# A decoder trunk with a mixture of experts on one core: the last projection with tokens stationary, a router by K quarters, fp32r counts, and three moved steps

## The chip, the core and the metric
The kernel runs on one core of a Trainium2 chip and is written engine by engine: TensorE (PE, with PEld for its weight loads), VectorE (DVE), ScalarE (ACT), GpSimd (POOL) and SyncE (SP, which mostly issues DMAs). Engines meet through semaphores. The metric is the device time of one execution in microseconds (us). Before the change three runs gave 897.81 us in the median (897.41 to 899.27).

## The reference
One layer over 320 tokens (256 of a prompt, 64 of 8 samples), width 2048, all fp32:

```
h = x @ w_in;  b, c, hc, u, v, p = split(h)
y = concat(b * conv3(c * hc), u * chunk_mix(LN(v)), pool(p))
x = LN(ALPHA * x + y @ w_out)                      # LN1
g = top1(softmax(x @ rg_w + rg_b))                 # one of 4 groups
e = top2(softmax((x @ re_w + re_b)[g]))            # 2 of its 4 experts
x = LN(ALPHA * x + sum_e gate_e * (silu(x @ w_gate_e) * (x @ w_up_e)) @ w_down_e)   # LN2
```

The outputs are x for all tokens and a few rows of state (the last rows of the convolution's and the pooling's inputs, the normalised v of the samples).

## The kernel before
**Projections.** A product with `w_in` or `w_out` is made from two parts of each operand: hi is the fp32r rounding, lo the rest, and hi*hi + hi*lo + lo*hi are summed in PSUM. A chunk of weights is 1 MB. SP loads it to `raw` (a ring of three, each load waits until the chunk three before it is used, `w_used`), ACT makes `w_hi` (L648), DVE `w_lo` (L656). `group_products` (L454) takes two chunks (8 K tiles by 256 columns each) with the weights stationary: per K tile and 128 columns three matmuls (L475 to L477) that stream the 320 tokens. A group fills two PSUM banks (pair g % 3); the result has the output columns on the partitions. Banks 6 and 7 are used in turn for transposes and small products (`tb_full`, `tb_free`). Groups 0 to 16 are `w_in`, groups 17 to 24 (G_O on) are `w_out`.

**The last projection.** Its input y is built in `tmp` two K tiles at a time by DVE, copied to `yT_hi` by ACT (`y_hi`, L680) and subtracted to `yT_lo` by DVE (`y_lo`, L816). The second half of K (tiles 8 to 15) comes first (HALF_O), since tiles 0 to 5 are only finished at its start. In ACT's program (`act_mixer`, g == 17) the order is: hi parts of chunks 34 and 35, `y_hi(2, 2)`, `y_hi(4, 2)`, the copies of z0 and z1 from banks 6 and 7 (L671), six small DMAs. On PE the transposes into z0 and z1 (L609) come right ahead of the projection. Since tokens are needed on the partitions afterwards, ACT copies each group to `mixT` (L793), PE turns it back (`out_tokens`, L624 and L629) and DVE adds it to ALPHA * x in `tok` (`residual`, L982 and L987) and takes its statistics (L996). Five of the expert units are loaded during this stage.

**LN1 and router.** LN1 is folded into the router: PE turns the unnormalised rows (48 transposes, L1142), ACT copies them to `zT` (L1356) with the root of the variance between its third and fourth copy, then PE multiplies all of K by the router's weights in four column strips (L1156, 32 instructions). DVE makes the choices. Cumulative counts of tokens per group and expert are fp32 matmuls with `before` and `ones` (`places_of`, L1169 to L1171, and L1183), the token that sits in each place comes from `group_slot` (L1177). DVE then writes `row` (L1448); POOL gathers the rows of group 0 from the copy in DRAM, `z_rows` (L1103), which has been stored by ACT (6 of 8 column groups) and SP (the last two).

**Experts.** The weights of 16 experts are 96 units of 2 MB (four of gate/up, two of down for each), in the order ORDER, in 11 slots. SP (`sp_experts`) issues units 5, 6, 9, 7, 10, 8 once the last projection is done, the fifth of them when `raw_made` is there, then unit 11 and so on, each when PE has used enough units (`ring_used`, `units_used`). For each expert PE turns the chosen rows (fill, L1206, with `order` from DVE's `pick`), multiplies by gate and up (L1270), turns the activation, multiplies by down (L1304) and combines with the gates (L1247). DVE's `normalise` (L1573) applies LN1 to the gathered rows, `finish` does LN2; its root is taken on ACT (`root`, L1405). POOL scatters the finished rows and gathers those of the group after the next one.

Of the kernel before, what the change touches and what calls it, by code (L numbers as in the profile page):

```python
# [37 lines left out]
def hybrid_trunk_kernel(nc, x_prompt, x_sample, state_conv, state_pool, w_in, conv_w, sgu_ln_g,  # L38
# [53 lines left out]
    BIG = 4096.0  # L92
# [30 lines left out]
    yT_hi = at("yT_hi", YT_HI0, [P, KT, NTOK], F32R)  # L123
    yT_lo = at("yT_lo", YT_LO0, [P, KT, NTOK], F32R)
# [35 lines left out]
    mixT = [at(f"mixT{s}", LATE + s * 2 * ROW, [P, 2, NTOK]) for s in range(3)]  # L160
# [9 lines left out]
    before = at("before", CO + 512, [P, P])  # L170
    ones = at("ones", CO + 1024, [P, P])
# [23 lines left out]
    group_slot = at("group_slot", G0 + 12 * KB, [P, 3, P])  # L195
# [39 lines left out]
    member = little("member", [P, 3, NR])  # L235
# [47 lines left out]
    small_out = S("small_out")  # L283
    copy_out = S("copy_out")
# [58 lines left out]
    HALF_O = (1, 0)  # L343
# [56 lines left out]
    def sp_program(sp):  # L400
# [18 lines left out]
        for o in range(16):  # L419
            c = 2 * G_O + o  # L420
            sp.wait_ge(w_used, c - RING + 1)
            h, col = HALF_O[o % 2], GW * (o // 2)
            sp.dma_start(raw[c % 3][:, :].rearrange("p (t n) -> p t n", t=CK),
                         wout_v[:, CK * h:CK * h + CK, col:col + GW]).then_inc(raw_full[c % 3], 16)
            if 4 <= o < 10:
                if o == 4:
                    sp.wait_ge(w_used, 2 * G_O)
                if o == 6:
                    sp.wait_ge(ylo_ready, 7)
                    sp.wait_ge(small_out, 16 * (4 + NB))  # L430
                load_half(sp, 2 + (o - 4) // 2, o % 2)

    def pool_program(pool):
        pool.memset(ident[:, :], 0.0).then_inc(pool_const, 1)
        pool.memset(ones[:, :], 1.0).then_inc(pool_const, 1)
# [7 lines left out]
        pool.affine_select(out=before[:, :], in_=ones[:, :], compare_op=ALU.is_gt, fill=0.0,  # L443
# [12 lines left out]
    def group_products(pe, g, acts, halves, turn=0, turns_at=0, wait_half=None, between=None):  # L456
# [6 lines left out]
        for n in range(2):  # L463
            if n and wait_half:
                pe.wait_ge(*wait_half)
# [47 lines left out]
    def pe_mixer(pe):  # L513
# [17 lines left out]
        X, Y = (xT_hi, xT_lo), (yT_hi, yT_lo)  # L531
# [81 lines left out]
        def out_tokens(k, turn=0):  # L613


            wait = pair_free[(G_O + k) % 3], (G_O + k) // 3 + 1 + turn
            pe.wait_ge(*wait)
            buf = mixT[k % 3]
            n = USE_O + 2 * k
            b, bank = bank_of(n, 3 * turn)  # L620
            b2, bank2 = bank_of(n + 1, 3 * turn)
            for i in range(2):
                for f in range(2):
                    last = pe.transpose(bank[:, GW * i + P * f:GW * i + P * (f + 1)],  # L624
                                        buf[:, f, P * i:P * (i + 1)], ident[:, :])
            last.then_inc(tb_full[b], 1)
            b, bank = b2, bank2
            for f in range(2):
                last = pe.transpose(bank[0:64, P * f:P * (f + 1)], buf[:, f, SEQ:NTOK], ident[:, :])  # L629
            last.then_inc(tb_full[b], 1)  # L630
# [28 lines left out]
    def store_z(eng, k, cols):  # L659

        for n in (USE_O + 2 * (k - 1), USE_O + 2 * (k - 1) + 1):
            b, full = tb(n)
            eng.wait_ge(tb_free[b], full)
# [3 lines left out]
    def act_mixer(act):  # L667
# [11 lines left out]
        def y_hi(first, n):  # L679
            act.activation(yT_hi[:, first:first + n, :], tmp[:, 0:n, :], ACT.Copy).then_inc(yhi_ready, 1)  # L680
# [105 lines left out]
        def copy_out_group(k, turn=0):  # L786
            g = G_O + k
            pair = g % 3
            act.wait_ge(w_used, 2 * g + 2 + 6 * turn)
            if k >= 3 or not isinstance(turn, int):  # L790
                b, full = tb(USE_O + 2 * k + 1)
                act.wait_ge(tb_full[b], full - 3 + 3 * turn)
            act.activation(mixT[k % 3][:, :, :], ps[:, 2 * pair:2 * pair + 2, 0:NTOK], ACT.Copy)\  # L793
               .then_inc(pair_free[pair], 1)

        with act.Fori(0, 2) as s:
            for i in range(3):
                split_hi(act, 2 * (G_O + 1 + i), s, 6)
                split_hi(act, 2 * (G_O + 1 + i) + 1, s, 6)
                copy_out_group(i, s)  # L800
        split_hi(act, 2 * G_END - 2)
        split_hi(act, 2 * G_END - 1)
        copy_out_group(6)
        store_z(act, 6, slice(0, 6 * GW))
        copy_out_group(7)

    def dve_mixer(dve):
# [6 lines left out]
        def y_lo(first, n, count):  # L814
            dve.wait_ge(yhi_ready, count)
            dve.tensor_tensor(yT_lo[:, first:first + n, :], tmp[:, 0:n, :],  # L816
                              yT_hi[:, first:first + n, :].bitcast(FP32), ALU.subtract)\
               .then_inc(ylo_ready, 1)
# [156 lines left out]
        def residual(k, turn=0):  # L975

            n = USE_O + 2 * k
            col = slice(GW * k, GW * (k + 1)) if isinstance(turn, int) else \
# [877 lines left out]
```

## Time and profile before

| | |
|---|---|
| median of three runs | 897.81 us |
| the profiled execution | 895.74 us |
| its span, first to last instruction | 894.0 us |
| PE busy | 837.3 us (94%) |
| DVE, ACT busy | 282.2 and 263.3 us |
| DMA: moved, mean rate | 267.80 MB, 300 GB/s |
| first part (`w_in`) | to 273 us |
| last projection | 273.4 to 391.1 us |
| LN1, router, first gather | 391 to 423 us |
| experts | 423 to 880 us |

The page gives the busy time of each engine and cuts the span in 40 slices of 22.35 us. The rows further down come from its views: a timeline gives start and length of merged neighbours ("x16" are 16 instructions) with the idle time before them and its releaser in brackets; windows give, for a stretch, the busy time and count of each engine, then the granted clock of PE (1.00 is 2.4 GHz, 0.50 is 1.2 GHz), the share of the DMA engines and GB/s; the chain of waits leads back from the last instruction.

### The profile page before, as it was taken

The numbers are of one execution on the slowest core, as the hardware profiler recorded it, in microseconds if no ns is written. First come the engines' busy times: TensorE is split into PE (matmuls) and PEld (weight loads), VectorE is DVE, ScalarE is ACT, GpSimd is POOL, SyncE is SP. The second block draws the span as 40 slices with busy tenths as digits, with TensorE's granted clock in tenths as the row PEclk, the third lists the DMA queues.
The fourth block names the chain that finished last, engine by engine and source line by source line (L and its number), as shares of the span: only waits on it lengthen the run. The fifth ranks groups of instructions, "written<-read, shape, count | busy, mean of one in ns | idle before, by whom it ended". The sixth has DMA issues, their size and how long they took to land.

```text
span 894.0 us, 11220 instructions
## 1 busy us (share of the span) xinstructions
PE 837.3 (94%) x4741; PEld 557.4 (62%) x4741; DVE 282.2 (32%) x388; ACT 263.3 (29%) x462; POOL 24.9 (3%) x41
## 2 busy tenths in 40 slices
PE   6999999999999999994999999998999989997993
PEld 6989999999999999984433333432333333333331
DVE  5383375335664444445000102043000330022203
ACT  5243332323223232321522332432223232222101
POOL 0000000000001000001000000000000000000000
PEclk9999999999999999995999999999999999999997
DMA  9644653654444884379898999999999999999980
GB/s 293 192 141 124 204 177 118 210 190 141 141 149 150 290 292 139 121 261 406 334 426 320 424 421 426 426 419 422 424 424 422 423 425 423 420 424 425 422 358 36
DMA packets 81148, 267.80 MB, mean 300 GB/s; under 512 B 5625, under 2 KB 58319, under 8 KB 59656
## 3 DMA queue, kind: packets, MB, share of 16 engines
q1 hardware_dynamic: 78042, 258.92, 74.7%
q0 software_dynamic: 1984, 5.31, 1.5%
q10 hardware_dynamic: 1078, 2.94, 1.0%
q8 instruction: 33, 0.54, 0.2%
q14 instruction: 11, 0.09, 0.0%
HBM read 263.07 MB, written 11.54 MB: 307 GB/s over the span
## 4 chain that ended last, share of the span: by engine, by line
PE 72%; DMA 15%; DVE 4%; ACT 4%; issue 2%; SPq 2%; POOL 0%; POOLq 0%; ACTq 0%; DVEq 0%
PE ps L1270 17%; PE ps L475 12%; PE ps L476 12%; PE ps L477 12%; PE ps L1304 9%; DMA down_w<-in_expert_w_down 4%; DMA gu_w<-in_expert_w_up 4%; DMA xg<-z_rows,row 4%; PE ps L1206 3%; DMA out<-xg,sample_row 3%; SPq L397 1%; ACT xT L1376 1%; DMA raw<-in_w_in 1%; DVE xg L1623 1%; PE ps L1247 1%
## 5 line engine op out<-in xcount | busy, mean ns | idle before, releaser
L1270 PE MATMUL ps<-gu_w,xT 128*64 128x512 f32 x1024 | 234.8, 600 | 7.7 <-DMA gu_w<-in_expert_w_up 6.7
L656 DVE TENSOR_TENSOR w_lo<-raw,w_hi 128x2048 fp32r<-128x2048 f32 x50 | 114.6, 2291 | 170.6 <-ACT w_hi L648 169.1
L475 PE MATMUL ps<-xT_hi,w_hi 128*128 128x320 f32 x512 | 159.2, 311 | 0.0
L477 PE MATMUL ps<-xT_hi,w_lo 128*128 128x320 f32 x512 | 158.2, 309 | 0.0
L476 PE MATMUL ps<-xT_lo,w_hi 128*128 128x320 f32 x512 | 158.2, 309 | 0.0
L1270 PEld LDWEIGHTS ps<-gu_w,xT 128*64 128x64 f32 x1024 | 71.5, 138 | 135.6 <-issue 131.2
L648 ACT ACTIVATE w_hi<-raw 128x2048 fp32r<-128x2048 f32 x49 | 93.8, 1915 | 207.9 <-DMA raw<-in_w_in 136.1
L1376 ACT ACTIVATE xT<-ps,gbT 128x64 f32<-128x64 f32 x256 | 82.4, 407 | 156.8 <-PE ps L1206 156.8
L1304 PE MATMUL ps<-down_w,aT 128*64 128x512 f32 x480 | 107.7, 601 | 4.5 <-ACT aT L1384 4.0
L475 PEld LDWEIGHTS ps<-xT_hi,w_hi 128*128 128x128 f32 x512 | 96.1, 188 | 0.5
L476 PEld LDWEIGHTS ps<-xT_lo,w_hi 128*128 128x128 f32 x512 | 96.1, 188 | 0.0
L477 PEld LDWEIGHTS ps<-xT_hi,w_lo 128*128 128x128 f32 x512 | 96.1, 188 | 0.0
L1645 DVE TENSOR_TENSOR a_sb<-ps,a_sb 128x256 f32<-128x256 f32 x16 | 6.8, 425 | 281.3 <-ACT a_sb L1428 281.3
L475 PE MATMUL ps<-yT_hi,w_hi 128*128 128x320 f32 x256 | 79.8, 312 | 0.7 <-DVE yT_lo L816 0.7
L1304 PEld LDWEIGHTS ps<-down_w,aT 128*64 128x64 f32 x480 | 33.3, 138 | 74.8 <-issue 61.9
L477 PE MATMUL ps<-yT_hi,w_lo 128*128 128x320 f32 x256 | 79.1, 309 | 0.0
L476 PE MATMUL ps<-yT_lo,w_hi 128*128 128x320 f32 x256 | 79.1, 309 | 0.0
L1206 PEld LDWEIGHTS ps<-order,xg 128*128 128x128 f32 x256 | 34.0, 196 | 57.5 <-issue 47.1
L1206 PE MATMUL ps<-order,xg 128*128 128x128 f32 x256 | 45.9, 305 | 8.6 <-DVE xg L1573 8.6
L475 PEld LDWEIGHTS ps<-yT_hi,w_hi 128*128 128x128 f32 x256 | 48.1, 188 | 0.9 <-DVE yT_lo L816 0.9
L476 PEld LDWEIGHTS ps<-yT_lo,w_hi 128*128 128x128 f32 x256 | 48.1, 188 | 0.0
L477 PEld LDWEIGHTS ps<-yT_hi,w_lo 128*128 128x128 f32 x256 | 48.0, 188 | 0.0
(257 smaller groups left out, 517.6 us busy)
## 6 DMA issues: line engine op xcount, KB each, us to landing
gu_w<-in_expert_w_gate SPq DMA_DIRECT2D x64, 1024.0 KB, 12.8
gu_w<-in_expert_w_up SPq DMA_DIRECT2D x64, 1024.0 KB, 15.0
down_w<-in_expert_w_down SPq DMA_DIRECT2D x32, 2048.0 KB, 19.6
raw<-in_w_in SPq DMA_DIRECT2D x34, 1024.0 KB, 5.3
raw<-in_w_out SPq DMA_DIRECT2D x16, 1024.0 KB, 5.3
tok<-in_x_prompt SPq DMA_DIRECT2D x2, 1024.0 KB, 6.4
z_rows<-tok ACTq DMA_DIRECT2D x2, 768.0 KB, 4.1
tok<-in_x_sample SPq DMA_DIRECT2D x1, 512.0 KB, 9.6
```

Source lines behind the costliest of these rows:

```text
L397: sp.dma_start(gu_w[s][:, n, :].rearrange("p (c f) -> p c f", c=4), src[:, e, h, c:c + 4, :])\
L475: pe.matmul(out, wh[:, t, col], hi[:, kt, :], start=(n == 0 and t == 0), stop=False)
L476: pe.matmul(out, wh[:, t, col], lo[:, kt, :], start=False, stop=False)
L477: last = pe.matmul(out, wl[:, t, col], hi[:, kt, :], start=False, stop=(n == 1 and t == CK - 1))
L648: act.activation(w_hi[k][:, :], raw[k][:, :], ACT.Copy).then_inc(hi_ready, 1)
L656: dve.tensor_tensor(w_lo[k][:, :], raw[k][:, :], w_hi[k][:, :].bitcast(FP32), ALU.subtract)\
L1206: last = pe.transpose(ps[:, fill_bank(e, j), P * c:P * (c + 1)], xg[g % 2][:, col:HD * (j // 2 + 1):HK], order[:, k, :])
L1247: last = pe.matmul(ps[:, ACC + 2 * h + q, :], gatedT[half, k, :], y[half, 512 * q:512 * (q + 1)], start=(k == 0), stop=(k == EG - 1))
L1270: last = pe.matmul(ps[C * side:C * (side + 1), GU, :], x, w[:, :, c, FH * side:FH * (side + 1)], start=(j == 0 and c == 0), stop=(j == PAI ...
L1304: last = pe.matmul(ps[C * side:C * (side + 1), out + q, :], turned[:, f % 2, f // 2, :], down_w[slot(i)][:, n, col:col + 512], start=(f == ...
L1376: last = act.activation(xT[e % 2][:, j, c, :], ps[:, fill_bank(e, j), P * c:P * c + C], ACT.Identity, bias=gbT[:, 1, j // 2, hc:hc + 1], s ...
L1623: dve.scalar_tensor_tensor(out=x[:, :], in0=x[:, :], scalar=zrstd[:, 0:1], in1=lnb[:, :], op0=ALU.mult, op1=ALU.add).then_inc(z_normed, 1)
```

## The change
- The last projection has the tokens stationary: `out_rows` goes over four quarters of 512 output columns; for each, four chunks of 4 K tiles by 512 columns. Tiles of 128 tokens: two of the prompt take three matmuls per K tile (hi with w_hi, lo with w_hi, hi with w_lo). The 64 sample tokens have their hi and lo parts side by side in `yT`, so that one stationary tile holds both, with two matmuls; DVE adds the two halves afterwards. The sums have the tokens on the partitions: no mixT copies, no `out_tokens`. `yT_hi` and `yT_lo` become one tensor with its K tiles placed by PLACE; `y_hi` and `y_lo` write it in pairs, `y_lo` in two pieces each.
- Residual and statistics go by quarters. PE waits for z0 and z1 to be read ahead of the first quarter, and for y's first six tiles ahead of the third chunk.
- Router: transposes go K quarter by K quarter, and the router's product of a quarter follows as soon as it is turned.
- `before`, `ones`, `member` and `group_slot` are fp32r, and the counts are fp32r matmuls; BIG is 512; the token numbers have a tensor of their own, `number`.
- SP waits for `xg_zero` 2 (POOL's clearing of the second xg, behind the first gather) ahead of unit 10.
- LN2's root is taken in `results`, ahead of the copies of gatedT and y, and the Silu table is called for once behind them; `pick` stands ahead of `normalise`.

```diff
+    yT = at("yT", YT_HI0, [P, KT, 2 * NTOK], F32R)
+    PLACE = (0, 1, 2, 8, 9, 10, 3, 4, 5, 11, 12, 13, 6, 7, 14, 15)
+    LO_S, LO_P = NTOK, 2 * NTOK - SEQ
-    HALF_O = (1, 0)
+    QUARTERS = (2, 3, 0, 1)
+    TO = 4
+    CO_W = CH // TO
+    QO = D // CO_W
+    ROW_BANKS = ((4, 5, 6), (0, 1, 7), (2, 3, 6), (4, 5, 7))
...
-        pe.wait_ge(ylo_ready, 4)
-        group_products(pe, G_O, Y, HALF_O, wait_half=(ylo_ready, 7))
-        with pe.Fori(0, 2) as s:
-            for i in range(3):
-                group_products(pe, G_O + 1 + i, Y, HALF_O, s, 3)
-                out_tokens(i, s)
-        group_products(pe, G_END - 1, Y, HALF_O)
-        out_tokens(6)
-        out_tokens(7)
+        wait_read(pe, "z0", "z1")
+        for q in range(QO):
+            out_rows(pe, q)
+
+    def out_rows(pe, q):
...
+        if q >= 2:
+            pe.wait_ge(rows_summed, 3 * (q - 1))
+        for n, kq in enumerate(QUARTERS):
+            c = 2 * G_O + 4 * q + n
+            if q == 0:
+                pe.wait_ge(ylo_ready, 4 if n < 2 else 7)
+            pe.wait_ge(lo_ready, c + 1)
...
+            for i in range(2):
+                out, rows = ps[:, ROW_BANKS[q][i], :], slice(P * i, P * (i + 1))
+                for t in range(TO):
+                    y = yT[:, PLACE[TO * kq + t], :]
+                    lo = slice(LO_P + P * i, LO_P + P * (i + 1))
+                    pe.matmul(out, y[:, rows], wh[:, t, :], start=(n == 0 and t == 0), stop=False)
+                    pe.matmul(out, y[:, lo], wh[:, t, :], start=False, stop=False)
+                    last = pe.matmul(out, y[:, rows], wl[:, t, :], start=False, stop=(n == 3 and t == TO - 1))
+                if n == 3:
+                    last.then_inc(rows_made, 1)
+            for t in range(TO):
+                out, both_parts = ps[:, ROW_BANKS[q][2], :], yT[:, PLACE[TO * kq + t], SEQ:LO_P]
+                pe.matmul(out, both_parts, wh[:, t, :], start=(n == 0 and t == 0), stop=False)
+                last = pe.matmul(out, both_parts, wl[:, t, :], start=False, stop=(n == 3 and t == TO - 1))
+            last.then_inc(w_used, 1)
...
+        for c in range(2 * G_O + 2, CHUNKS1 - 1):
+            split_hi(act, c)
+        store_z(act, 3, slice(0, 3 * CO_W))
+        split_hi(act, CHUNKS1 - 1)
...
+        def residual(q):
+
+            col = slice(CO_W * q, CO_W * (q + 1))
+            for i in range(2):
+                dve.wait_ge(rows_made, 2 * q + i + 1)
+                dve.scalar_tensor_tensor(out=tok[:, i, col], in0=tok[:, i, col], scalar=ALPHA,
+                                         in1=ps[:, ROW_BANKS[q][i], :], op0=ALU.mult, op1=ALU.add)\
+                   .then_inc(rows_summed, 1)
+                dve.wait_ge(rows_summed, 3 * q + i + 1)
+                steps.inc(dve.bn_stats(xstats[:, i, q, :], tok[:, i, col]))
+            dve.wait_ge(w_used, 2 * G_O + 4 * (q + 1))
+            bank = ROW_BANKS[q][2]
+            link(dve.scalar_tensor_tensor(out=tok[0:64, 2, col], in0=tok[0:64, 2, col], scalar=ALPHA,
+                                          in1=ps[0:64, bank, :], op0=ALU.mult, op1=ALU.add))
+            dve.tensor_tensor(tok[0:64, 2, col], tok[0:64, 2, col], ps[64:128, bank, :], ALU.add)\
+               .then_inc(rows_summed, 1)
...
             if i == SLOTS + 1:
                 sp.wait_ge(raw_made, 1)
+                sp.wait_ge(xg_zero, 2)
...
+        turn_z(0)
+        turn_z(1)
+        pe.wait_ge(rw_ready, 4)
+        route(0)
+        turn_z(2)
+        route(1)
+        turn_z(3)
+        route(2)
         pe.wait_ge(sums_ready, 2)
...
+        route(3).then_inc(lgT_made, 1)
...
         def results(e, turned):
             if e < NE - 1:
                 turned_a(e)
+            if e % EG == 0 and e:
+                root(e // EG - 1)
             if turned:
...
             if k == 1 and g:
-                root(g - 1)
+                act.activation(spare[:, :], vstd[:, 0:1], ACT.Silu)
...
                 if g < NG - 1:
+                    pick(g + 1)
                     normalise(g + 1)
-                    pick(g + 1)
```

## Rows read from the trace of the kernel before
**Rows 1.** The page's DMA share in 40 slices, and a window of the expert stage.
```profile
DMA  9644653654444884379898999999999999999980
...
800.00:840.00 40.00, 34.08 (x160) 12.83 (x160) 14.69 (x16) 10.51 (x24) 1.98 (x2) 1.00 1.01 421
```
**Rows 2.** Timeline of PE, the end of the expert stage.
```profile
824.64 3.65 PE L1270 MATMUL ps<-gu_w,xT 128*64 128x512 f32 x16 [2.52 <-DMA gu_w<-in_expert_w_up]
...
868.94 3.65 PE L1304 MATMUL ps<-down_w,last_aT 128*64 128x512 f32 x16 [0.16 <-DMA down_w<-in_expert_w_down]
```
**Rows 3.** The chain of waits, near its end: start, length, what.
```profile
835.54 33.27 DMA down_w<-in_expert_w_down
```
**Rows 4.** Windows with a low DMA share, and SP's timeline where it ends.
```profile
427.00:429.00 2.00, 2.00 (x12) 0.70 (x10) 0.00 (x0) 0.00 (x0) 0.00 (x0) 1.00 0.19 74
...
475.00:480.00 5.00, 5.00 (x26) 1.86 (x24) 0.00 (x0) 1.29 (x4) 2.14 (x4) 1.00 0.71 290
...
481.22 4.55 SPq L1073 DMA_DIRECT2D down_w<-in_expert_w_down  x2
```
**Rows 5.** Timeline of PE: the first fill of xT.
```profile
423.17 1.97 PE L1206 MATMUL ps<-order,xg 128*128 128x128 f32 x8 [5.00 <-DVE xg L1573]
```
**Rows 6.** Timeline of PE and ACT where the last projection begins.
```profile
272.81 0.82 PE L609 MATMUL ps<-ident,zlast 128*18 128x128 f32 x6
273.38 0.39 PE L475 MATMUL ps<-yT_hi,w_hi 128*128 128x320 f32 x1
...
280.31 0.83 ACT L671 ACTIVATE z_out<-ps 18x512 f32<-18x512 f32 x2
```
**Rows 7.** Timeline of PE around an idle stretch, and a window of it.
```profile
621.35 1.09 PE L1206 MATMUL ps<-order,xg 128*128 128x128 f32 x4 [2.70 <-DVE xg L1573]
622.36 4.78 PE L1270 MATMUL ps<-gu_w,xT 128*64 128x512 f32 x16
...
622.00:624.00 2.00, 2.00 (x7) 0.56 (x7) 2.00 (x2) 1.29 (x4) 0.00 (x0) 0.50 1.00 418
```
**Rows 8.** Timeline of PE in the last projection: the first and last of 19 starts.
```profile
299.75 0.31 PE L477 MATMUL ps<-yT_hi,w_lo 128*128 128x320 f32 x1
...
302.39 0.31 PE L477 MATMUL ps<-yT_hi,w_lo 128*128 128x320 f32 x1
```
**Rows 9.** Timeline of PE, one of eight groups of spreads; a gate_up in the chain.
```profile
562.33 0.39 PE L1221 MATMUL ps<-ln_lo,one_of 16*128 16x512 f32 x1
562.56 0.39 PE L1220 MATMUL ps<-ln_hi,one_of 16*128 16x512 f32 x1
562.80 0.39 PE L1221 MATMUL ps<-ln_lo,one_of 16*128 16x512 f32 x1
...
632.01 3.58 PE ps L1270 x16
```
**Rows 10.** Timeline of PE and DVE behind the last projection.
```profile
390.79 0.31 PE L477 MATMUL ps<-yT_hi,w_lo 128*128 128x320 f32 x1
...
391.57 0.69 DVE L982 SCALAR_TENSOR_TENSOR tok<-tok,ps 128x512 f32<-128x512 f32 x1 [7.63 <-PE ps L624]
...
394.83 5.76 PE L1142 MATMUL ps<-ident,tok 128*128 128x128 f32 x48 [1.25 <-DVE tok L987]
```
**Rows 11.** Timeline of ACT and PE in the router.
```profile
397.41 3.62 ACT L1356 COPY zT<-ps 128x512 f32<-128x512 f32 x9
...
401.18 2.36 PE L1156 MATMUL ps<-zT,rw 128*32 128x320 f32 x32
...
409.04 1.52 PE L1177 MATMUL ps<-facts,group_slot 128*128 128x1 f32 x6 [0.92 <-DVE group_slot L1491]
```
**Rows 12.** Timeline of SP, POOL and DVE at the first gather; all four gathers' landing.
```profile
407.51 0.33 SPq L1073 DMA_DIRECT2D down_w<-in_expert_w_down  x1
...
411.77 1.12 POOL L1103 DMA_INDIRECT xg<-z_rows,row  x1 [18.72 <-DVE row L1448]
...
419.88 0.55 DVE L1541 TENSOR_TENSOR group_slot<-slots,group_rank 128x384 f32<-128x384 f32 x1
422.30 1.53 DVE L1573 TENSOR_SCALAR xg<-xg,told 128x1024 f32<-128x1024 f32 x2 [1.88 <-DMA xg<-z_rows,row]
...
DMA to landing us min/median/max: 9.2/10.3/11.3
```

More of the change, by code:

```diff
@@ L91, in hybrid_trunk_kernel @@
     NR = NG + NE
-    BIG = 4096.0
+    BIG = 512.0
     KB = 1024
@@ L234, in hybrid_trunk_kernel @@
     place_in = little("place_in", [P, 3, NR])
-    member = little("member", [P, 3, NR])
+    member = little("member", [P, 3, NR], F32R)
+    number = little("number", [P, 4], F32R)
     chosen = little("chosen", [P, 3, NE])
@@ L454, in pool_program, with group_products @@
                            channel_multiplier=1).then_inc(pool_const, 1)
-    def group_products(pe, g, acts, halves, turn=0, turns_at=0, wait_half=None, between=None):
+    def group_products(pe, g, acts, halves, turn=0, turns_at=0, between=None):
         hi, lo = acts
@@ L611, in pe_mixer @@
             last.then_inc(tb_full[b], 1)
[L613 to L621, printed above, removed]
-            for i in range(2):
[L623 to L630, printed above, removed]
@@ L679, in y_hi @@
         def y_hi(first, n):
-            act.activation(yT_hi[:, first:first + n, :], tmp[:, 0:n, :], ACT.Copy).then_inc(yhi_ready, 1)
+            for k in range(0, n, 2):
+                last = act.activation(yT[:, two_of(first + k), 0:NTOK], tmp[:, k:k + 2, :], ACT.Copy)
+            last.then_inc(yhi_ready, 1)
         for i, (t0, m) in enumerate(TILES):
@@ L815, in y_lo @@
             dve.wait_ge(yhi_ready, count)
-            dve.tensor_tensor(yT_lo[:, first:first + n, :], tmp[:, 0:n, :],
-                              yT_hi[:, first:first + n, :].bitcast(FP32), ALU.subtract)\
-               .then_inc(ylo_ready, 1)
+            for k in range(0, n, 2):
+                two = two_of(first + k)
+                steps.inc(dve.tensor_tensor(yT[:, two, LO_P:2 * NTOK], tmp[:, k:k + 2, 0:SEQ],
+                                            yT[:, two, 0:SEQ].bitcast(FP32), ALU.subtract))
+                last = dve.tensor_tensor(yT[:, two, LO_S:LO_P], tmp[:, k:k + 2, SEQ:NTOK],
+                                         yT[:, two, SEQ:NTOK].bitcast(FP32), ALU.subtract)
+                if k < n - 2:
+                    steps.inc(last)
+            last.then_inc(ylo_ready, 1)
             dve.wait_ge(ylo_ready, count)
@@ L1006, in dve_mixer @@
+        for c in range(2 * G_O + 4, CHUNKS1):
+            split_lo(dve, c)
+            if (c - 2 * G_O) % 4 == 1:
+                residual((c - 2 * G_O) // 4 - 1)
         dve.wait_ge(rw_in, 16 * 4)
@@ L1176, in pe_router @@
         for i, (t0, m) in enumerate(TILES):
-            last = pe.matmul(ps[:, INFO, 0:1], group_slot[0:m, i, :], facts[0:m, i, 0, 0:1],
+            last = pe.matmul(ps[:, INFO, 0:2], group_slot[0:m, i, :], number[0:m, i:i + 2],
                              start=(i == 0), stop=(i == 2))
```

149 lines of the change are left out of this document (54 added, 95 removed).

## The prediction
> **What bounds the kernel now.** I read four views, in this order. First the page's line of DMA share: from slice 23 of 40 to slice 38 it stands at 9, so in the expert stage the weights keep the DMA engines full, at 421 GB/s also in a stretch where TensorE (PE) is busy for 34 of 40 us [rows 1]. Second, the end of the PE timeline: from 787 us on gate_up starts late, each time released by a gu_w transfer, and the last expert's down_w lands at 868.9 just as PE arrives [rows 2]. The chain of waits says the same: that last down_w was issued 33 us before it landed, so it stood in a full queue [rows 3]. The end is therefore set by the DMA stream. Third, I looked for the last place where this stream itself ran dry, since whatever is late there is late at the end. The windows give 427 to 431 (share 0.19) and, last, 475 to 485 (share 0.71, then about 0.6) [rows 4]. The second gap ends when SP issues unit 20 of ORDER, at 481.22; its wait, `units_used(20)` = 12, is for PE to have consumed gate_up(2, 1), so the stream is paced by PE's progress there. So **a shift of PE's start in the expert stage is passed on whole to the end**, and nothing that PE gains after 485 us is. Fourth, I followed the timeline back from PE's first fill of xT, at 423.17, which waits for the first gather (normalise at 422.30) [rows 5, 12]. The sum is thus the shift of that start.
>
> **When the last projection starts.** Before, its first matmul runs at 273.38, right behind the z transposes, and its first chunk (7 us) runs while DVE and ACT still finish y's first six tiles [rows 6]. In the changed `pe_mixer`, `wait_read(pe, "z0", "z1")` stands ahead of `out_rows(0)`, since tile 2 of the first quarter takes bank 6. But ACT copies z0 and z1 only behind its `y_hi(4, 2)`: 280.31 to 281.14 [rows 6]. Queued behind the waiting PE instruction is the whole projection. So it starts at about 281.2. The new wait `ylo_ready` 7 only before the third chunk is free of cost (y_lo in two pieces ends about 0.1 us later than 281.3, the third chunk starts near 298), and the 0.9 us that PE stood there before is inside the absolute times used here. Chunks 34 to 36 are split long before they are needed, since the stall gives DMA, ACT and DVE 8 us.
>
> PE idles nearly 8 us there, and the granted clock should fall. The nearest row is the wait for the second group's rows: after 2.7 us idle the clock is 0.50 (1.2 of 2.4 GHz), four transposes take 1.09 us and a gate_up 4.78, where the same take 0.71 and 3.65 later [rows 7]: 0.4 + 1.1, say 1.6 us with the first instructions. Bounds 0 and 2.5 us; I take **1.6**, since the idle stretch is longer.
>
> **The matmuls.** Before, 768 of 320 columns, 18 starts in 2.64 us, 0.1467 us apart [rows 8]. After, 4 quarters x 4 chunks x (2 tiles x 4 x 3 + 4 x 2) = 512 of 512 columns, fp32r. The trace has 512-column fp32r matmuls where the layer norm's vectors are spread (lines 1220, 1221): in eight groups of four the last starts 0.45 to 0.47 us behind the last but two, mean 0.464, so 0.2319 us each [rows 9]. Its weight loads (0.19) hide as now. The nearest other row is gate_up, 16 in 3.58 us, 0.2238 [rows 9], fp32 in two column halves. I take 0.2319, the same type and width; 0.2238 is the low end, 0.2347 (0.1467 x 512/320) the high one. So the last matmul starts at 281.2 + 1.6 + 511 x 0.2319 = 401.3, against 390.79 [rows 10], and ends at 401.7 against 391.1: **+10.6 us** (low -4.1, high +1.4). The 48 transposes of out_tokens and ACT's mixT copies go away; what they cost before is inside the 391.1 that I compare with.
>
> A rule speaks about this term. The Trainium skill (TensorE: Matmul & The Clock Gate, Back-to-back issue gap) gives columns / 2.4 GHz + 2.5 ns at full clock, 215.8 ns for 512 columns, by which the projection would end 8.2 us sooner. The trace differs on both widths (146.7 against 135.8 ns; 231.9 against 215.8), so the row decides.
>
> **From the last matmul to the logits.** Before: copy of mixT, four transposes, residual, again for group 7, first z transpose at 394.83, all 48 done at 400.6, then 32 route instructions in 2.36 us, done 403.54: 12.4 us behind the last matmul [rows 10, 11]. After: rows of tiles 0 and 1 are final 4.6 and 1.8 us before the end, and their residuals (0.69 + 0.68) are hidden by the matmuls still running. Tile 2 has two links behind the last matmul (0.69 each with their gaps [rows 10]): +1.6. Then statistics (0.68), aggregates, the root: ACT is free for the remaining nine zT copies at about +4.0 and needs 3.6 for them [rows 11]. On PE's side: q1 transposes to 3.5, route 0 to 4.2, q2 transposes to 5.7, route 1 behind the sixth copy to 6.3, q3 transposes (12 x 0.12) to 7.8, route 2 to 8.4, the sums to 9.1, route 3 (a quarter of 2.36) to 9.8, and 0.2 for the turns between tile shapes: 10.0. PE is later than ACT here. **-2.4 us**; bounds -3.4 (each turn free and the sums hidden) and 0 (each of four turns into 32-column tiles and back costs 0.3).
>
> The Trainium skill (TensorEngine Tiling (Array Packing), Key Properties) says that changing the tiling mode drains TensorE, and this change makes four such changes of one. No row prices a drain.
>
> **The counts in fp32r.** An fp32 matmul is two instructions; six of them take 1.52 us [rows 11], so about 0.22 for each that goes. Rank: 6 to 3, first: 6 to 3: -0.65 each, on the way to the gather, **-1.3**. Places and counts: 12 to 6, -1.3, only on the way to `told`. Bounds: 0 (narrow fp32r no quicker) to -3.3 for all. BIG = 512, `number`, the bitcasts and DVE's two small copies more cost nothing: they lie under chunks 48 and 49 or are single elements.
>
> So the gather is issued at 411.77 + 10.6 - 2.4 - 1.3 = 418.7 [rows 12]. z_stored is no later relative to it.
>
> **The gather and the units behind it.** SP's i == SLOTS + 1 now also waits for `xg_zero` 2: behind the gather's issue (1.12) and a 1.83 us memset; before, the two units went out at 405 and 407.5 [rows 12]. All later units queue behind them on SP, but those wait for PE until 436 anyway. Their slots (gate_up(2,0), down(0)) are read only after 465. What does it give the gather? Units 5, 6, 7, 9 (8.4 MB) and 0.66 MB of z are issued from 401.8 and need 21.8 us at 415 GB/s: the engines are full until 424, and unit 10 (issued near 421.6) keeps them full. The gather's data thus never meets an empty queue. The four gathers of before landed 9.2 to 11.3 us after issue, the first in 10.5 [rows 12]; with gate/up units as the only rivals, as now, it was the 9.2. I take 9.4, bounds 7 and 10.5. Landing: 428.1 against 422.3. DVE comes free for normalise(0) at 420.43 + 10.6 - 2.4 - 2.6 = 426.0 [rows 12], earlier. **PE's start moves by +5.8 us.** The stream's later start is no second delay: it begins 10.6 us later but had 8 us of gaps before 485, unit 19 is then through at about 481, and unit 20 comes at 487.
>
> **Behind 485 us.** `root(g)` ahead of y's copy frees DVE's last scale by 2.4 us, `pick` ahead of `normalise` takes 1.5 us out of PE's wait for the second and third gather. Hidden by the full DMA stream: 0. gatedT's copy now stands behind root on ACT; it is needed by fill(7, 0), 3 us later: 0. The last group's root and finish do not change.
>
> **Sum.** 895.74 (profiled execution; span 894.0 and 1.7 around it) + 5.8 = 901.5; the median of the runs lies 2.1 above the profiled one, so **903.6 us**.
>
> **Rivals.**
> - The gather meets little rivalry (unit 7 is nearly through) and lands within 7 us: then DVE's 426.0 decides, +3.8: 901.6. Chance 0.15. For it: it is what the new wait does; against: 9 MB ahead of it.
> - 512-column matmuls as gate_up's, 0.2238: -4.1, 899.5. Chance 0.08. For it: K is 128 rows in both; against: other type.
> - **Faster**: the projection streams one column per cycle of the granted 2.4 GHz, 0.2133 us for 512. Place: the 512 matmuls; price 512 x 0.0186 = 9.5 us; it turns the sign below 0.2206 us, and passes 0.2% below 0.217. 894.1. Chance 0.07; no row of either width has it. By the Trainium skill's figure above (TensorE: Matmul & The Clock Gate) it would be 895.4.
> - The four turns of route cost what the interleaving saves: 906.0. Chance 0.09.
> - The end is PE's after all and root and pick pay: about -6, 897.6. Against: nine waits for gu_w from 787 on. Chance 0.05.
> - The change doesn't do what it says, in that PE is not held for z0 and z1 (ACT's copies in time): -9.3, 894.3. Chance 0.04: the order of ACT's program is plain.
> - The forecast, 903.6: 0.52.
>
> About 0.2% (1.8 us) is what a measurement of this kernel can tell from no change. The range goes from 898.8 (takes in 0.2238 or the quick gather) to 907.0 (clock 2.5, spacing 0.2347, or costly turns); some 0.16 lies below, 0.04 above. Faster 0.11 (the two cases that end below 896), same 0.12 (897.6 and most of 899.5), slower 0.77.
>
> **What would show it.** PE idle from 273.5 to about 281.2 with ACT L671 as the releaser, and the clock at 0.50 after; starts 0.232 apart; last projection matmul near 401.3; route's last instruction 10 us behind it; gather issued near 418.7 and landing over 9 us later; the first gap of the stream (427 to 431) gone, the second still ended by unit 20, near 487; waits for gu_w at the end not smaller. The prediction is wrong if the spacing is under 0.22, if PE starts at 273, or if the end doesn't move with PE's first gate_up.

## The result, and the profile after

The changed kernel takes 902.51 us (median of 13 runs, 899.62 to 905.68), the kernel before 898.25 (13 runs, 896.38 to 900.93). The ratio is 1.0045 [1.0032, 1.0058]: slower by 4.3 us, over the 0.2% that a measurement can tell. The forecast was 903.6. The profiled executions are 6.3 apart (895.74 and 902.07); the section on the variation between profiles shows why that is more than the medians say.

The page of the changed kernel: span, granted clock, DMA share, the costliest group. Waits for gu_w take 12.8 us in all (6.7 in the kernel before).
```profile
span 900.3 us, 10467 instructions
...
PEclk9999999999998999996899999999999999999997
DMA  9644644554552675539898999999999999999980
...
L1281 PE MATMUL ps<-gu_w,xT 128*64 128x512 f32 x1024 | 236.9, 605 | 13.8 <-DMA gu_w<-in_expert_w_up 12.8
```
Its timelines of PE and ACT where the last projection begins (start, length, what; in brackets the idle time before, and its releaser), and windows (busy time of PE, PEld, DVE, ACT, POOL, then granted clock, DMA share, GB/s).
```profile
272.78 0.82 PE L618 MATMUL ps<-ident,zlast 128*18 128x128 f32 x6
280.12 0.77 PE L648 MATMUL ps<-w_hi,yT 128*128 128x512 f32 x1 [6.51 <-ACT z_out L686]
...
279.18 0.83 ACT L686 ACTIVATE z_out<-ps 18x512 f32<-18x512 f32 x2
...
280.00:282.00 2.00, 1.88 (x5) 1.53 (x6) 0.20 (x1) 0.02 (x1) 1.48 (x2) 0.50 0.17 37
282.00:284.00 2.00, 2.00 (x7) 1.61 (x6) 0.00 (x0) 1.60 (x1) 1.86 (x6) 0.61 0.37 85
284.00:286.00 2.00, 2.00 (x11) 1.62 (x10) 1.58 (x1) 0.31 (x1) 0.00 (x0) 1.00 0.04 4
```
Where [rows 6] had the projection right behind the z transposes, PE now stands for 6.51 us, until ACT has copied z0 and z1, and then works at half clock until about 283.6.

PE from the end of the projection to the row counts, POOL's issue of the gather, DVE at its landing.
```profile
395.86 0.39 PE L650 MATMUL ps<-w_lo,yT 128*128 128x512 f32 x1
...
397.68 0.40 PE L656 MATMUL ps<-w_lo,yT 128*128 128x512 f32 x1
397.92 1.06 PE L1144 MATMUL ps<-ident,tok 128*128 128x128 f32 x8
...
402.51 1.75 PE L1144 MATMUL ps<-ident,tok 128*128 128x128 f32 x12
...
407.89 0.75 PE L1152 MATMUL ps<-zT,rw 128*32 128x320 f32 x8
...
413.70 0.89 PE L1188 MATMUL ps<-number,group_slot 128*128 128x2 f32 x3 [1.45 <-DVE group_slot L1504]
...
415.81 1.11 POOL L1106 DMA_INDIRECT xg<-z_rows,row  x1 [15.78 <-DVE row L1461]
...
422.60 0.55 DVE L1554 TENSOR_TENSOR group_slot<-slots,group_rank 128x384 fp32r<-128x384 f32 x1
426.62 1.53 DVE L1586 TENSOR_SCALAR xg<-xg,told 128x1024 f32<-128x1024 f32 x2 [3.47 <-DMA xg<-z_rows,row]
```
Against [rows 10 to 12] the last matmul starts 6.9 us later (397.68), the gather goes out 4.0 later (415.81) and is read 4.3 later (426.62). DVE was done at 423.15 and waited 3.47 us for it.

PE and SP in the expert stage, with windows of the stream.
```profile
427.49 1.97 PE L1217 MATMUL ps<-order,xg 128*128 128x128 f32 x8 [6.59 <-DVE xg L1586]
429.99 5.50 PE L1281 MATMUL ps<-gu_w,xT 128*64 128x512 f32 x16 [0.53 <-ACT xT L1387]
...
470.44 8.78 PE L1315 MATMUL ps<-down_w,aT 128*64 128x512 f32 x32
...
486.92 4.55 SPq L1076 DMA_DIRECT2D down_w<-in_expert_w_down  x2
...
434.00:436.00 2.00, 2.00 (x13) 0.87 (x10) 0.00 (x0) 0.00 (x0) 0.00 (x0) 1.00 0.22 82
...
485.00:490.00 5.00, 5.00 (x26) 1.86 (x24) 0.00 (x0) 1.29 (x4) 0.10 (x1) 1.00 0.46 125
...
875.28 3.65 PE L1315 MATMUL ps<-down_w,last_aT 128*64 128x512 f32 x16
```
The fill of xT starts 4.32 later than [rows 5], unit 20 goes out 5.70 later than [rows 4], the last expert's down starts 6.34 later than [rows 2]. The stream still has two gaps, at 434 to 436 (share 0.22) and at 485 to 490 (0.46), the second ended by unit 20 as before.

### The profile page after: what moved, and what is told of

It reads as the page before. It is cut to its first block, busy times and chain, and to the rows that moved or that the text cites. A ratio compares the mean times of both kernels' runs of the same rounds, so it can differ in the third digit from the quotient of the medians.

```text
span 900.3 us, 10467 instructions
## 1 busy us (share of the span) xinstructions
PE 837.8 (93%) x4425; PEld 535.6 (59%) x4425; DVE 285.2 (32%) x387; ACT 258.9 (29%) x458; POOL 24.8 (3%) x41
## 4 chain that ended last, share of the span: by engine, by line
PE 69%; DMA 18%; DVE 6%; ACT 3%; issue 2%; SPq 2%; POOL 0%; POOLq 0%; ACTq 0%; DVEq 0%
PE ps L1281 16%; PE ps L484 8%; PE ps L485 8%; PE ps L486 8%; DMA gu_w<-in_expert_w_up 7%; PE ps L1315 7%; DMA down_w<-in_expert_w_down 4%; DMA xg<-z_rows,row 4%; PE ps L648 3%; PE ps L649 3%; PE ps L650 3%; PE ps L1217 3%; DMA out<-xg,sample_row 3%; PE ps L656 2%; PE ps L655 2%
## 5 line engine op out<-in xcount | busy, mean ns | idle before, releaser
L1281 PE MATMUL ps<-gu_w,xT 128*64 128x512 f32 x1024 | 236.9, 605 | 13.8 <-DMA gu_w<-in_expert_w_up 12.8
L648 PE MATMUL ps<-w_hi,yT 128*128 128x512 f32 x128 | 50.7, 396 | 6.5 <-ACT z_out L686 6.5
L649 PE MATMUL ps<-w_hi,yT 128*128 128x512 f32 x128 | 50.4, 394 | 0.0
L650 PE MATMUL ps<-w_lo,yT 128*128 128x512 f32 x128 | 50.3, 393 | 0.0
L1414 ACT COPY y_sb<-ps 128x1024 f32<-128x1024 f32 x15 | 15.2, 1012 | 87.3 <-PE ps L1315 87.3
L648 PEld LDWEIGHTS ps<-w_hi,yT 128*128 128x128 f32 x128 | 24.4, 191 | 11.9 <-ACT z_out L686 6.8
L1258 PE MATMUL ps<-y_sb,gatedT 64*128 64x512 f32 x120 | 29.8, 615 | 0.0
```

Of the source, the lines that this page charges most:

```text
L648: pe.matmul(out, y[:, rows], wh[:, t, :], start=(n == 0 and t == 0), stop=False)
L649: pe.matmul(out, y[:, lo], wh[:, t, :], start=False, stop=False)
L650: last = pe.matmul(out, y[:, rows], wl[:, t, :], start=False, stop=(n == 3 and t == TO - 1))
L1281: last = pe.matmul(ps[C * side:C * (side + 1), GU, :], x, w[:, :, c, FH * side:FH * (side + 1)], start=(j == 0 and c == 0), stop=(j == PAI ...
```

## Why two profiles of one kernel differ, and how the runs are compared

A second profiled execution of the kernel before took 897.65 us (span 895.7), 1.9 longer than the first. Its rows show where.

> The kernel before once more, for a second profile. In the first its first gate_up takes 4.14 us, in the profiles of the changed kernel and its variants 4.4 to 5.8. Theory: this is where in time the clock's rise happens to fall, and differs between executions of one kernel; here it takes 4.2 to 5.8 and the start of the last projection lies anywhere in 273 to 277. Rival: it is a property of the old router (PE idles less), and takes 4.1 to 4.2 again.

Timeline of PE, kernel before, second execution.
```profile
273.98 0.82 PE L609 MATMUL ps<-ident,zlast 128*18 128x128 f32 x6
...
424.24 1.97 PE L1206 MATMUL ps<-order,xg 128*128 128x128 f32 x8 [5.18 <-DVE xg L1573]
426.73 4.87 PE L1270 MATMUL ps<-gu_w,xT 128*64 128x512 f32 x16 [0.53 <-ACT xT L1376]
...
466.55 8.79 PE L1304 MATMUL ps<-down_w,aT 128*64 128x512 f32 x32
...
870.73 3.65 PE L1304 MATMUL ps<-down_w,last_aT 128*64 128x512 f32 x16 [0.20 <-DMA down_w<-in_expert_w_down]
```
Two things vary, and the change touches neither. All that lies ahead of the last projection ends up to 3.4 us earlier or later (the z transposes start at 272.7 to 276.2). And the granted clock is at its lower level, 1.2 GHz, for part of the first gate_up (3.65 us at full clock, 4.14 to 5.80 as a rule) and, in some executions, of the first down (7.09, or 8.3 to 8.8). So I read each kernel from its own z transposes:

| kernel | z transposes | fill of xT, behind them | gate_up 1, down 1 | unit 20 | last down | median us | ratio to before |
|---|---|---|---|---|---|---|---|
| before | 272.81 | 150.36 | 4.14, 8.26 | 481.22 | 868.94 | 898.25 | |
| before, again | 273.98 | 150.26 | 4.87, 8.79 | 483.04 | 870.73 | | |
| after | 272.78 | 154.71 | 5.50, 8.78 | 486.92 | 875.28 | 902.51 | 1.0045 |
| no_gate | 272.87 | 154.42 | 5.80, 7.09 | 485.32 | 874.53 | 902.77 | 1.0049 |
| old_ln2 | 274.01 | 154.72 | 5.75, 7.09 | 486.74 | 875.03 | 902.68 | 1.0051 |
| route_last | 275.85 | 154.73 | 4.43, 8.57 | 488.89 | 877.27 | 904.20 | 1.0063 |
| counts32 | 274.10 | 155.77 | 5.10, 8.78 | 488.91 | 877.47 | 903.56 | 1.0054 |
| more_behind | 272.72 | 151.20 | 5.61, 8.78 | 483.48 | 872.65 | 899.08 | 1.0012 |
| z_late | 274.56 | 147.29 | 5.57, 8.78 | 481.35 | 870.47 | 894.84 | 0.9959 |
| both_edits | 274.08 | 143.84 | 4.51, 8.65 | 476.31 | 864.60 | 890.28 | 0.9906 |
| both_warm | 272.96 | 145.34 | 3.65, 7.09 | 474.15 | 862.00 | 893.10 | 0.9940 |
| before_stall | 276.16 | 159.07 | 5.71, 7.09 | 493.18 | 881.54 | 907.48 | 1.0093 |

What to see: the one program that was profiled twice repeats in the third column within 0.1 us (150.36 and 150.26), and three that differ only off this path lie within 0.3 us (154.71, 154.42, 154.72). From the fill to unit 20 there are 55.9 us in all twelve, once what gate_up takes over 3.65 and down over 7.09 is taken off (and up to 0.5 of the transposes ahead of that down at lower clock): after, 59.43 - 1.85 - 1.69 = 55.89; z_late, 59.50 - 1.92 - 1.69 = 55.89. From unit 20 to the last down there are 387.7 to 389.2. No run moves unit 20 by itself, but the clock does part of that: from the fill to the last down the profiles differ by 5.0 us (443.70 to 448.73), from unit 20 to it by 1.5. Nearly the whole difference between the kernels thus lies in the third column: 154.71 - 150.3 = **4.4 us**, and the medians differ by 4.3. The other 2 us of the two profiled executions are the clock (3.5 us of it after, 2.1 before, but 2.9 before, again) and 0.7 of the last stretch.

## The experiments

**1. The wait for z0 and z1, moved (z_late) and put into the kernel before (before_stall).** Theory: the stall ahead of the projection is most of the loss. Rival: the loss is in the matmuls or behind them.
```
-        wait_read(pe, "z0", "z1")
         for q in range(QO):
 ...
         elif q == 1:
+            wait_read(pe, "z1")
 ...
+            if q == 0 and n == 0:
+                wait_read(pe, "z0")
             for t in range(TO):
```


> The changed kernel, with PE's wait for z0 moved behind the first 24 matmuls of the last projection and the one for z1 to the second quarter. Theory (the stall ahead of the projection is carried to the end one to one): the projection starts at 273.4 instead of 280.1, the clock stays at 2.4 GHz, its last matmul starts near 390, gather, first fill and unit 20 each move by about -7.5 us against the changed kernel, and so does the end: near 895, ratio to the kernel before 0.995 to 0.997. Rival (the loss lies in the 512-column matmuls and in the gather that meets full queues, and the stall is absorbed by later waits): the end moves by less than 3 us, near 900.

Timeline of PE in z_late.
```profile
275.13 0.48 PE L648 MATMUL ps<-w_hi,yT 128*128 128x512 f32 x1
...
281.56 0.50 PE L657 MATMUL ps<-w_hi,yT 128*128 128x512 f32 x1 [0.71 <-ACT z_out L688]
...
421.85 1.97 PE L1219 MATMUL ps<-order,xg 128*128 128x128 f32 x8 [6.55 <-DVE xg L1588]
```
894.84 us (10 runs), 0.9959 [0.9943, 0.9975]. The first 24 matmuls run under ACT's work, the wait behind them is 0.71 us, and the fill comes 7.42 us earlier behind the z transposes than after. The medians differ by 7.7. Without that one wait the change is a gain of about 3 us over the kernel before (3.0 at the fill, 3.2 by the medians of that comparison, 894.84 for 898.02).
```
         pe.wait_ge(ylo_ready, 4)
+        wait_read(pe, "z0", "z1")
         group_products(pe, G_O, Y, HALF_O, wait_half=(ylo_ready, 7))
```


> The kernel before, with one line more: PE waits for z0 and z1 to be read ahead of the last projection. Theory: the first matmul moves from 273.4 to about 281.2, the first group runs at half clock for some 3 us, the last one ends 8 us later (the 0.9 us wait inside the first group goes), and the end moves by +8, near 906. Rival (the weight stream had 8 us of gaps before 485 us, so a later start is absorbed there): +0 to +3 us.

Timeline of PE in before_stall.
```profile
276.16 0.82 PE L609 MATMUL ps<-ident,zlast 128*18 128x128 f32 x6
284.75 0.61 PE L475 MATMUL ps<-yT_hi,w_hi 128*128 128x320 f32 x1 [7.78 <-DVE yT_lo L817]
...
435.23 1.97 PE L1207 MATMUL ps<-order,xg 128*128 128x128 f32 x8 [5.02 <-DVE xg L1574]
```
907.48 us (6 runs), 1.0093 [1.0070, 1.0116]: 9.5 by the medians (907.48 for 898.02), 8.8 at the fill. The profile names DVE's yT_lo as the releaser, since that ended at 284.66, 0.1 us behind the copies of z (284.55); the edit adds only the wait for the copies, and without it PE did not stand there. The stall is 284.75 - 276.16 - 0.57 = 8.0 us. From the first to the last matmul there are 118.1 us (284.75 to 402.84) for 117.4 before: the low clock adds about 1.6 (it lasts until 288.3, with starts 0.27 us apart in place of 0.15), and the wait for y inside the first group, which cost 0.8 in the profile before, is gone. Both directions agree: this wait costs 7.4 us in the new order and 8.8 in the old one, clock included, and nothing behind it takes any of that back.

**2. The gather's landing: without the new wait on xg_zero (no_gate), and with one unit more behind it (more_behind).** Theory: what counts is how many megabytes are queued when the gather goes out. Rival: rivals that are issued behind it count too.
```
                 sp.wait_ge(raw_made, 1)
-                sp.wait_ge(xg_zero, 2)
```


> The changed kernel without SP's wait for the second clearing of xg ahead of unit 10. Theory (the gather meets full queues either way): the gather lands 10.3 to 11.3 us after its issue as against 10.8 with the wait, the first fill moves by less than 0.7 us, the end by less than 1 us. Rival (the wait does shield the gather): landing later by 2 us or more and the end by as much.

The units go out at 410.22 and 414.78, ahead of the gather (415.96), and it still lands in 10.4 us, for 10.8 in after, where it goes out at 415.81. 902.77 us (12 runs), 1.0049 [1.0031, 1.0066], for 1.0045. The new wait buys nothing. Units 5, 6, 9 and 7 were already queued (issued from 398.1 on); 4 MB more ahead of the gather did not delay it. So my theory does not hold as it was put: it isn't the number of megabytes in the queue.
```
-            if i == SLOTS + 1:
+            if i == EARLY + 2:
                 sp.wait_ge(raw_made, 1)
```


> The changed kernel with unit 7 behind the gather too, so that 6.3 MB of units and 0.7 MB of z are ahead of it and not 8.4: about 17 us of the stream from 399 us, empty at 416 to 417, when the gather's data start. Theory: the gather lands 4 to 6 us after its issue (near 421), DVE's chain (423.1) then decides, the first fill comes 3.4 us earlier, and the end 2 to 3.4 us earlier, near 899, unless the hole in the stream costs it. Rival (10 us is the gather's own time, not rivalry): landing stays over 9 us and nothing moves.

Timelines of POOL, DVE and PE in more_behind.
```profile
415.87 1.12 POOL L1106 DMA_INDIRECT xg<-z_rows,row  x1 [15.85 <-DMA z_rows<-tok]
...
423.05 1.53 DVE L1586 TENSOR_SCALAR xg<-xg,told 128x1024 f32<-128x1024 f32 x2
...
423.92 1.97 PE L1217 MATMUL ps<-order,xg 128*128 128x128 f32 x8 [3.04 <-DVE xg L1586]
```
A window of after, then the same of more_behind.
```profile
418.00:420.00 2.00, 0.66 (x3) 0.67 (x4) 1.14 (x7) 0.00 (x0) 0.75 (x1) 0.50 0.97 406
```
```profile
418.00:420.00 2.00, 0.68 (x4) 0.68 (x4) 1.12 (x7) 0.00 (x0) 0.81 (x1) 0.50 0.68 242
```
The gather, issued at 415.87, lands in 6.8 us (5.8 in both_edits): DVE no longer waits for it and sets the fill itself. 899.08 us (12 runs), 1.0012 [0.9994, 1.0029], 3.4 less than after. One unit of 2 MB (unit 7, issued at 402.5 in after, at 418.9 here) moved behind it takes 3.5 us off the fill. The windows show what differs: in after the DMA engines stay full while the gather is under way (share 0.94 to 1.05 from 414 to 426), here they have room from 416 to 422 (0.89, 0.68, 0.85). That this room is what lets the gather land sooner agrees with both runs; how the engines share their time between the two queues no run shows.

**3. The two edits together (both_edits), and with PE kept warm (both_warm).** The first has the diffs of z_late and more_behind, the second two products more, which run while the gather is under way.


> The changed kernel with PE's waits for z0 and z1 moved (as in z_late) and unit 7 behind the gather too (as in more_behind). Theory (both act on one chain whose shift is passed on whole, so they add): against the changed kernel -7.5 and -3.5 us at PE's first fill and at unit 20, the end near 891 to 892, ratio to the kernel before 0.992 to 0.993. Rival (with the earlier start the weight stream itself becomes the limit before 485 us, since unit 7 starts 15 us later): the end stays at 894 to 895, as z_late alone.

890.28 us (6 runs, 888.83 to 891.78), 0.9906 [0.9884, 0.9928]: faster than both kernels, and 0.9% faster than the one before. The fill comes 10.87 us earlier behind the z transposes than after; 7.42 + 3.51 = 10.93 is the sum of the two edits. They are independent, since each takes a wait off a different part of one chain.
```
         info(0, FACTS, info_made)
+        pe.wait_ge(order_ready, 1)
+        for n in range(2):
+            pe.matmul(ps[:, GU, :], ident[:, :], order[:, :, :].rearrange("p k s -> p (k s)"),
+                      start=True, stop=True)
         fill(0, 0)
```


> both_edits with two idle products more on PE (512 columns fp32, ident by order, into a bank that gate_up clears) once order is there, while the gather is still under way. They add nothing to the output. Theory (the first gate_up of 5.5 us is the clock at 1.2 GHz after the router's idle stretches): the clock rises before or early in the first gate_up, which takes 3.6 to 4.6 us in place of 5.6, and the end comes up to 1.5 us earlier than both_edits. Rival: the two products delay the first fills by about as much as they give, no difference.

Timeline of PE in both_warm.
```profile
418.30 1.91 PE L1219 MATMUL ps<-order,xg 128*128 128x128 f32 x8
420.75 3.65 PE L1283 MATMUL ps<-gu_w,xT 128*64 128x512 f32 x16 [0.53 <-ACT xT L1393]
```
The rival came. The clock has risen by the first gate_up (3.65 us for 4.51), but the two products run until 418.3, and normalise had begun at 415.85, by which the fill could have started at 416.7 (0.87 behind it, as in both_edits). So the fill is 1.5 us later behind the z transposes. 893.10 us (6 runs), 0.9940 [0.9918, 0.9963]: the median is 2.8 us higher than that of both_edits, and the intervals just overlap. No gain can be shown; whether shorter products would give one was not tried.

**4. The counts in fp32 again (counts32).** All four count products on bitcasts of the same tiles:
```
-            pe.matmul(out, before[:, :], member[:, :, cols], start=True, stop=False)
+            pe.matmul(out, before[:, :].bitcast(FP32), m32, start=True, stop=False)
```


> The changed kernel with the matmuls of places_of, of the first tokens and of the counts in fp32 again, two instructions each. Theory (fewer instructions are what fp32r saves there): rank, first and places take 0.4, 0.6 and 1.3 us longer, the gather is issued 1.0 us later, unit 20 moves by +1.0 us, the end near 903.5 (+1.0 against the changed kernel). Rival (narrow fp32r no quicker): no difference in these three steps.

Timeline of PE and DVE in counts32.
```profile
413.30 0.60 PE L1182 MATMUL ps<-member,before 128*128 128x12 f32 x2 [1.73 <-DVE member L1489]
...
414.85 0.17 DVE L1504 SCALAR_TENSOR_TENSOR group_rank<-ps,member 128x12 f32<-128x12 f32 x1 [0.46 <-PE ps L1184]
...
415.67 1.53 PE L1190 MATMUL ps<-number,group_slot 128*128 128x2 f32 x6 [0.93 <-DVE group_slot L1506]
```
The same step in after, then in the second profile of the kernel before, where the counts are fp32 too.
```profile
412.89 0.17 DVE L1502 SCALAR_TENSOR_TENSOR group_rank<-ps,member 128x12 f32<-128x12 f32 x1
```
```profile
407.98 0.39 PE L1169 MATMUL ps<-member,before 128*128 128x12 f32 x2 [1.73 <-DVE member L1474]
...
409.11 0.17 DVE L1489 SCALAR_TENSOR_TENSOR group_rank<-ps,member 128x12 f32<-128x12 f32 x1
```
From the first count to group_rank 1.55 us for 1.13 (411.76 to 412.89 in after), and 1.53 for 0.89 at the row numbers: 0.42 + 0.64 = 1.06. The fill is 1.06 later behind the z transposes, the median 1.05 higher. In ratios (1.0054 [1.0033, 1.0075] for 1.0045) this is below what the runs tell apart; the profiles show it.

The 0.42 is not a saving that fp32r always brings. In after DVE has work of its own until 412.85 and doesn't wait for the counts; all eight profiles with fp32r have 1.12 or 1.13 us here. In the second profile of the kernel before the granted clock stays at 2.4 GHz until 408.7, and the fp32 counts also take 1.13 (407.98 to 409.11). In its first profile and in counts32 the clock has fallen just before (at 406.2 and 411.4), the counts take 1.55, and DVE waits 0.46 for them. So at this step fp32 costs something only at 1.2 GHz; the 0.64 at the row numbers was seen at 1.2 GHz alone.

**5. The router's products last (route_last).** All 48 transposes, then the sums, then the 32 router products, as before the change:
```
-        turn_z(0)
-        turn_z(1)
+        for q in range(4):
+            turn_z(q)
 ...
-        route(0)
-        turn_z(2)
 ...
+        for q in range(3):
+            route(q)
         route(3).then_inc(lgT_made, 1)
```


> The changed kernel with all 48 transposes ahead of the 16 route products, as before the change, the order of tiles kept. Theory (the interleaving hides three quarters of route behind the transposes and copies): the logits are ready 1 to 2 us later behind the last projection matmul than the 10.6 us of the changed kernel, and gather, unit 20 and end by as much, near 904. Rival (each turn between tile shapes costs, and the transposes wait for ACT's copies in the interleaved order): 0 or earlier.

Timelines of PE and POOL in route_last.
```profile
401.52 1.06 PE L1144 MATMUL ps<-ident,tok 128*128 128x128 f32 x8
403.18 5.69 PE L1144 MATMUL ps<-ident,tok 64*128 64x64 f32 x40 [0.60 <-DVE tok L996]
...
409.47 2.36 PE L1152 MATMUL ps<-zT,rw 128*32 128x320 f32 x32
...
419.01 1.11 POOL L1106 DMA_INDIRECT xg<-z_rows,row  x1 [15.38 <-DMA z_rows<-tok]
```
My theory of 1 to 2 us falls. From the first transpose to the last router product there are 10.3 us (401.52 to 411.83), for 10.7 with the quarters interleaved (397.92 to 408.64). The gather goes out 17.5 us behind the first transpose for 17.9, and the fill stands at 154.73 for 154.71. The median, 904.20 (6 runs), 1.0063 [1.0041, 1.0084], is 1.7 higher, but its interval overlaps the changed kernel's, and in the profile the router gives none of it: the z transposes alone are 3.1 us later. So working in K quarters brings nothing that can be shown. One more thing is close here: in this profile the gather's releaser is the landing of the last rows of z in DRAM, not `row`. In after that landing (401.3 + 13.3 = 414.6) comes only 0.3 us ahead of `row` (ready at 414.86), so a quicker router would soon wait for it.

**6. The LN2 root and pick back in their old places (old_ln2).**
```
-            if e % EG == 0 and e:
-                root(e // EG - 1)
 ...
-                    pick(g + 1)
                     normalise(g + 1)
+                    pick(g + 1)
```


> The changed kernel with LN2's root behind y's copy again, no call for the Silu table, and pick behind normalise. Theory (from unit 20 on the weight stream is full, and what PE waits between groups is made up before the last units land): PE waits 1 to 3 us longer before the fills of groups 2 and 3, and the end does not move: last down_w 388 us behind unit 20's issue as in the others, time within 1 us of the changed kernel's. Rival (PE is as much the bound as the stream): +3 to +6 us, near 907.

Timeline of PE in old_ln2.
```profile
627.28 1.09 PE L1217 MATMUL ps<-order,xg 128*128 128x128 f32 x4 [3.16 <-DVE xg L1584]
...
738.31 0.69 PE L1217 MATMUL ps<-order,xg 128*128 128x128 f32 x4 [1.38 <-DVE xg L1584]
...
875.03 3.65 PE L1315 MATMUL ps<-down_w,last_aT 128*64 128x512 f32 x16
```
PE waits for the second and third group's rows again, 3.16 and 1.38 us; with the change these are 0 and 0.90. Yet unit 20 (486.74 for 486.92), the last down (875.03 for 875.28) and the time (902.68, 7 runs, 1.0051 [1.0027, 1.0076]) are the same. What PE gains there it gives back waiting for gu_w: 4.0 us in old_ln2, 12.8 in after.

## Why the prediction was right, and where its terms were not

The time was right to 1.1 us, and so were the sign and the chain that carries the loss to the end, but the closeness is partly luck. The forecast was a shift of 5.8 us on a first median of 897.81; measured were 4.3 on 898.25, and the errors of the terms are 4.1 us in one direction and 2.6 in the other. By its steps:

- **The end is the DMA stream's, paced last by unit 20.** Right, and now shown: 387.7 to 389.2 us from unit 20 to the last down while unit 20 itself moves by 19 us. That nothing PE gains behind it counts is shown by old_ln2. But of the stream's two gaps the first was to go, and it only became shorter (share 0.22 at 434 to 436, for 0.19 from 427 to 431 before).
- **Start of the projection, 281.2.** 280.12. The mechanism was right (releaser z_out). ACT copies z 1.1 us earlier than before (279.18 for 280.31), which I had held fixed. The change itself does this. The second chunk of `w_out`, whose hi part stands ahead of the copies on ACT, is issued at the same time (265.94 for 265.96) but lands in 5.0 us for 6.2, and ACT starts on it 1.6 to 1.9 us ahead of the z transposes in all nine profiles with the new order, for 0.5 to 0.6 in the three with the old one. Its pieces are 512 columns (2 KB) where they were 256 (1 KB); that this is the reason is likely, but no run separates it.
- **Clock, 1.6.** 280.12 + 511 x 0.2261 = 395.66 for 397.68: 2.0 us, inside the bounds.
- **Spacing, 0.2319: the term that was mis-sized.** From 299.76 to 397.68 there are 433 intervals of 0.2261 us. Over 511 that is 3.0 us less. The row that I took, [rows 9], is of the same type and width but has 16 rows of stationary data and stands alone in groups of four; gate_up's 0.2238, taken as the low end, was nearer. The full-speed rival (0.2133) didn't come. Nor does the Trainium skill's figure (TensorE: Matmul & The Clock Gate, Back-to-back issue gap) hold for these products: 215.8 ns for 512 columns, which the section calls the gap of an isolated product, with about 131 ns for a sustained stream; both are below the 226.1 measured. The last matmul started at 397.7, not 401.3.
- **Router, -2.4.** From the end of the last matmul (398.07) to the last product 10.6 us for 12.4: -1.85. But part of that saving was to come from the interleaving, and that step failed: route_last does without it (10.15 us from the end of the last matmul). What is saved is the wait ahead: the first z transpose starts 0.24 us behind the start of the last matmul, where before it stood 4.04 behind [rows 10], since residuals are now hidden. From there to the last product the changed kernel needs 10.7 us, 2.0 more than before (394.83 to 403.54). The transposes are slower, but not by the interleaving: twelve take 1.75 us in after, and in route_last 40 in a row take 5.69, which is 1.71 for twelve, against 1.44 at the rate of [rows 10]. Why they are slower in both orders is open. The Trainium skill (TensorEngine Tiling (Array Packing), Key Properties) has each change of tiling mode drain TensorE. The order with four such turns is 0.4 us slower than the one with a single turn (10.7 for 10.3), some 0.1 net for each; what a drain costs by itself no run here separates.
- **Counts, -1.3 on the path.** -1.06. Rank gave 0.42, not 0.65, since DVE's own work then sets that step, and in the second profile of the kernel before it would have given nothing (experiment 4). What is saved in the other counts lies off this path. The forecast also has the stores of z no later than the gather's issue, relative to it. That came out otherwise: the last one landed 3.3 us ahead of `row` before (407.5 for 410.83), 0.3 ahead after. It cost nothing yet.
- **Landing, 9.4.** 10.8. I took the shortest of [rows 12], for having gate/up units alone as rivals. Before, units 10 and 8 went out 6.8 and 4.3 us ahead of the first gather and it took 10.5; with them behind it takes 10.8, and in no_gate, with them ahead again, 10.4. So they make no difference on either side, and the kind of rivals was no reason to take 9.4. The rival in which it lands within 7 us needs one unit fewer ahead: more_behind (6.8).
- **The first gate_up at low clock** was not in my sum. It costs in both kernels. With the first down it takes 2.1 to 2.9 us in the three profiles of the old order and 2.1 to 3.7 in the eight of the new one without added products; these ranges overlap, and so few profiles can't tell whether the new order loses more there.

Together: -1.1 + 0.4 - 3.0 + 0.55 + 0.25 + 1.4 = -1.5, so the fill moved by 4.3, not 5.8. The medians agree. What was mis-sized most is the spacing, then the landing.

## What to carry to other kernels

A wait at the head of a long PE loop cost its full length and the clock after it here: place it in front of the first instruction that needs the buffer (here 24 matmuls later: 7.4 us). In a kernel whose end is a saturated DMA stream, find the last gap of the stream and the instruction that ends it; in this one, what came ahead of it counted in full and what came behind it for nothing. For a gather that meets a full stream, look at the DMA share while it is under way: taking one unit out of that stretch took 4.0 us off the landing (10.8 to 6.8), while two units issued just ahead of the gather or just behind it made no difference.

## What the chip did that I had not expected

- Back to back, 512-column fp32r matmuls on 128 rows start 226.1 ns apart, 0.442 ns for a column; at 320 columns 146.7, 0.458 for a column. The wider form streams 512 x 512 = 262,144 columns for 768 x 320 = 245,760, so that 115.8 us stand against 112.7; what it saves is the work of `out_tokens` between the groups.
- Behind the same gap of 1.81 us ahead of the first down the granted clock falls in some executions and not in others. Windows of after, then of no_gate.
```profile
470.00:472.00 2.00, 2.00 (x10) 0.86 (x11) 0.00 (x0) 0.59 (x1) 0.00 (x0) 0.82 1.03 430
472.00:474.00 2.00, 2.00 (x8) 0.53 (x6) 0.00 (x0) 0.00 (x0) 0.00 (x0) 0.50 0.98 410
```
```profile
472.00:474.00 2.00, 2.00 (x12) 0.59 (x10) 0.00 (x0) 0.00 (x0) 0.00 (x0) 1.00 1.00 418
```
It is 1.7 us (8.78 for 7.09) that no edit decides, as much as the smaller effects of this study.
